# Adaptive-norm modulation in a 1-core block kernel: the two condition vectors become the stationary operand, the weights stream 512 wide, and three norm sums move between the weight tiles

## What is computed

```python
# end of the first block
x = x + 0.5 * swiglu_ffn(rmsnorm(x, norm_ffn2), ffn2_w_in, ffn2_w_out)
x = rmsnorm(x, norm_final)
# start of the second block; c is the condition of x, c_ctx that of ctx (256 positions)
m_x = split(silu(c)     @ mod_w + mod_b, 6)      # mod_w is 1024 x 6144
m_c = split(silu(c_ctx) @ mod_w + mod_b, 6)
h_x = rms_norm(x,   norm1_g) * (1.0 + m_x[1]) + m_x[0]
h_c = rms_norm(ctx, norm1_g) * (1.0 + m_c[1]) + m_c[0]
z_x = h_x @ w_in
z_c = h_c @ w_in
# then a recurrent mixer, neighbourhood attention, a merge, and 16 routed experts (top 2)
```

## Time and profile before

| what | value |
|---|---|
| median of 3 runs | 4668.71 us |
| the profiled execution's own time | 4666.49 us |
| its span, first to last instruction | 4664.9 us |
| PE busy | 3958.7 us (85%), 16948 instructions |
| PEld busy | 2824.8 us (61%) |
| DVE, ACT, POOL busy | 1965.5, 1160.9, 915.5 us |
| mean granted TensorE clock | 0.864 of full |
| modulation, L903: 768 matmul rows | 164.0 us |
| HBM read and written | 362.01 MB, 33.03 MB |

### The profile page before, as it was taken

One profiled execution on the slowest core, in us unless ns is written; L12 is line 12 of the kernel. 1 busy time (PEld: TensorE's weight loads), 2 busy tenths in 40 slices (PEclk: granted clock), 3 DMA queues, 4 the chain that ended last, 5 costly groups with the idle time before them and its releaser, 6 DMA issues.

```text
span 4664.9 us, 48689 instructions
## 1 busy us (share of the span) xinstructions
PE 3958.7 (85%) x16948; PEld 2824.8 (61%) x16948; DVE 1965.5 (42%) x2791; ACT 1160.9 (25%) x1552; POOL 915.5 (20%) x513
## 2 busy tenths in 40 slices
PE   8998888677499989999798766588898979969996
PEld 6875555333144458789454444587888864457775
DVE  2101554588600021100201333656666550159997
ACT  4421443323200033310101122111111010046663
POOL 4442000000000024420000000101101000049996
PEclk9999999888799999985898555788888979979998
DMA  2224111111022222234111000000000002349996
GB/s 102 94 89 172 45 45 40 39 51 49 19 76 76 73 70 92 90 127 153 50 59 45 9 18 25 1 0 0 0 0 0 0 0 89 110 172 357 358 356 242
DMA packets 106808, 395.84 MB, mean 85 GB/s; under 512 B 11680, under 2 KB 11696, under 8 KB 106112
## 3 DMA queue, kind: packets, MB, share of 16 engines
q1 hardware_dynamic: 95040, 347.42, 21.4%
q0 software_dynamic: 8400, 35.61, 2.0%
q10 hardware_dynamic: 3312, 12.06, 0.6%
HBM read 362.01 MB, written 33.03 MB: 85 GB/s over the span
## 4 chain that ended last, share of the span: by engine, by line
PE 67%; DVE 21%; issue 7%; ACT 3%; DVEq 1%; POOL 1%; DMA 1%; ACTq 0%; POOLq 0%; SPq 0%; PEldq 0%
PE psum L1379 9%; PE psum L827 7%; PE psum L197 5%; PE psum L196 5%; PE psum L198 5%; DVE er_r L1885 5%; PE psum L459 4%; DVE mem L775 4%; PE psum L903 4%; PE psum L945 3%; PE psum L1703 2%; PE psum L1097 2%; PE psum L469 1%; PE psum L1079 1%; PE psum L834 1%
## 5 line engine op out<-in xcount | busy, mean ns | idle before, releaser
L186 POOL TENSOR_TENSOR ring_r<-ring,whi 128x1024 fp32r<-128x1024 f32 x132 | 319.4, 2436 | 924.9 <-ACT whi L181 924.9
L1379 PE MATMUL psum<-mem 128*128 128x128 f32 x3520 | 462.3, 295 | 4.4
L1379 PEld LDWEIGHTS psum<-mem 128*128 128x128 f32 x3520 | 446.0, 210 | 16.9 <-DVE mem L1559 11.5
L1885 POOL TENSOR_TENSOR er_r<-er,eh 128x1024 fp32r<-128x1024 f32 x134 | 426.0, 3216 | 50.2 <-ACT eh L1873 50.2
L1885 DVE TENSOR_TENSOR er_r<-er,eh 128x1024 fp32r<-128x1024 f32 x134 | 367.8, 2784 | 0.0
L196 PE MATMUL psum<-ffn_xh,ring_r 128*128 128x512 f32 x704 | 279.3, 397 | 24.7 <-DVE xn_r L210 24.7
L681 PE MATMUL psum<-xn,ring 128*128 128x512 f32 x512 | 238.1, 629 | 69.2 <-ACT mem L717 64.8
L197 PE MATMUL psum<-ffn_xh,whi 128*128 128x512 f32 x704 | 281.2, 399 | 0.0
L198 PE MATMUL psum<-xn_r,whi 128*128 128x512 f32 x704 | 279.2, 397 | 0.0
L1873 ACT ACTIVATE eh<-er 128x1024 fp32r<-128x1024 f32 x268 | 262.5, 1071 | 10.0 <-DMA er<-experts 9.4
L681 PEld LDWEIGHTS psum<-xn,ring 128*128 128x128 f32 x512 | 103.0, 203 | 204.2 <-issue 199.0
(11 more groups left out here) (458 smaller groups left out, 6904.5 us busy)
## 6 DMA issues: line engine op xcount, KB each, us to landing
ring<-stream SPq DMA_DIRECT2D x359, 512.0 KB, 3.3
er<-experts SPq DMA_DIRECT2D x276, 512.0 KB, 6.0
xs_dram<-zero_row POOLq DMA_DIRECT2D x1, 12288.0 KB, 38.3
xs<-xs_dram SPq DMA_DIRECT2D x23, 512.0 KB, 6.6
ys_dram<-y_t ACTq DMA_DIRECT2D x23, 512.0 KB, 6.4
mem<-rpb POOLq DMA_DIRECT2D x8, 512.0 KB, 4.4
resid<-x_t SPq DMA_DIRECT2D x1, 2048.0 KB, 7.8
spill<-resid POOLq DMA_DIRECT2D x1, 2048.0 KB, 6.6
```

Source lines behind the costliest of these rows:

```text
L186: pool.tensor_tensor(ring_r[:, s, :, :], ring[:, s, :, :], f(whi[:, s, :, :]), ALU.subtract).then_inc(w_lo, 1)
L1379: ins = pe.matmul(psum[:, bank, q * n:(q + 1) * n], lhs[:, q, :], rhs if rhs is two_ident else rhs[:, q, :], start=True, stop=True)
L1885: eng.tensor_tensor(er_r[:, at, :], er[:, at, :], f(eh[:, at, :]), ALU.subtract).then_inc(done, 1)
```

## The change

It changes the modulation's product and what surrounds it, in six places:

- **Roles.** The two conditions are now stationary (128 rows, 2 columns) and 512 columns of weights move. There are 12 groups of 4 slabs; each group gives a 2 x 512 row in PSUM bank 0 or 1, by turns, from 8 products. The host lays the 48 slabs out anew (same size and number).
- **Rows to columns.** ACT copies each 2 x 512 row to `modrow` (L939). When all 12 are there, PE turns them by 48 transposes into bank 6 (L918), where DVE finds them as before.
- **Earlier start.** PE waits for the second of DVE's 8 additions to `resid`, not the eighth.
- **Sums between groups.** `norm_pe(pe, 3)` stands after 2 groups, `norm_pe(pe, 4)` and the context's sums (now L930) after 7. ACT's squares and roots and DVE's reciprocals are put in matching places.
- **Interleaved norm.** `mod_norm_dve` writes its additions between its multiplications, for norm 4 and for norm 5; the reciprocal is its own function, `rstd_dve`.
- **Finer waits.** The first `in2` tile waits for `xn` tile by tile, and the wait for the context's `hc` stands at the first tile that reads it.

```diff
-        def mod_pe(pe):
-            pe.wait_ge(resid_ready, 3 * DT)
-            pe.wait_ge(cs_dve, 1)
-            with pe.Fori(0, 12) as i:
-                for j in range(4):
-                    w = use_slab(pe, "mod", j, i, 4)
-                    for k in range(DT):
-                        ins = pe.matmul(psum[:, 6, bass.ds(i * 8 + 2 * j, 2)], w[:, k, :], cs[:, k:k + DT + 1:DT],
                                         start=k == 0, stop=k == DT - 1)
                     ins.then_inc(slab_used, 1)
+        def mod_rows(pe, groups):
+            for n in groups:
+                if n >= 2:
+                    pe.wait_ge(row_act, n - 1)
+                for j in range(4):
+                    w = use_slab(pe, "mod", 4 * n + j).rearrange("p a c -> p (a c)")
+                    for kk in range(2):
+                        k = 2 * j + kk
+                        ins = pe.matmul(psum[0:2, n % 2, :], cs[:, k:k + DT + 1:DT], w[:, kk * T:(kk + 1) * T],
+                                        start=k == 0, stop=k == DT - 1)
+                    ins.then_inc(slab_used, 1)
+        def mod_turn(pe, groups):
+            for n in groups:
+                pe.wait_ge(row_act, n + 1)
+                for m in range(4 * n, 4 * n + 4):
+                    ins = pe.transpose(psum[:, 6, 2 * m:2 * m + 2], modrow[:, m * P:(m + 1) * P], ident[0:2, 0:2])
+            return ins
+        def mod_and_norms_pe(pe):
+            pe.wait_ge(resid_ready, 2 * DT + 2)
+            pe.wait_ge(cs_dve, 1)
+            mod_rows(pe, (0, 1))
+            norm_pe(pe, 3)
+            mod_rows(pe, range(2, 7))
+            norm_pe(pe, 4)
...
+            ins.then_inc(cn_pe, 1)
+            mod_rows(pe, range(7, 12))
+            mod_turn(pe, range(12)).then_inc(turned, 1)
+        def mod_and_norms_act(act):
+            def take(groups):
+                for n in groups:
+                    act.wait_ge(slab_used, SLAB_AT["mod"] + 4 * n + 4)
+                    act.activation(modrow[:, n * T:(n + 1) * T], psum[0:2, n % 2, :], ACT.Copy).then_inc(row_act, 1)
...
         def block2_pe(pe):
-            norm_pe(pe, 4)
...
-            pe.wait_ge(xn_ready, 5 * DT)
-            pe.wait_ge(cn_dve, 1 + 2 * DT)
...
+                        if t == 0:
+                            pe.wait_ge(xn_ready, 4 * DT + k + 1)
...
+                        if u == 0:
+                            pe.wait_ge(cn_dve, 1 + 2 * DT)
...
         def block2_dve(dve):
-            dve.wait_ge(slab_used, SLAB_AT["mod"] + 48)
+            rstd_dve(dve, 4)
+            dve.wait_ge(cn_act.sem, cn_act.at(0, "std"))
+            dve.reciprocal(stdc, stdc).then_inc(cn_dve, 1)
+            dve.wait_ge(turned, 1)
```

More of the change, by code:

```diff
@@ L893, in hybrid_block_kernel @@
         spilled = sem("spilled")
-        def mod_pe(pe):
-            pe.wait_ge(resid_ready, 3 * DT)
-            pe.wait_ge(cs_dve, 1)
-            with pe.Fori(0, 12) as i:
+        modrow = mem[0:2, 0:48 * P]
+        row_pe = sem("mod_row_pe")
+        row_act = sem("mod_row_act")
+        turned = sem("mod_turned")
+        def mod_rows(pe, groups):
+            for n in groups:
+                if n >= 2:
+                    pe.wait_ge(row_act, n - 1)
                 for j in range(4):
-                    w = use_slab(pe, "mod", j, i, 4)
-                    for k in range(DT):
-                        ins = pe.matmul(psum[:, 6, bass.ds(i * 8 + 2 * j, 2)], w[:, k, :], cs[:, k:k + DT + 1:DT],
+                    w = use_slab(pe, "mod", 4 * n + j).rearrange("p a c -> p (a c)")
+                    for kk in range(2):
+                        k = 2 * j + kk
+                        ins = pe.matmul(psum[0:2, n % 2, :], cs[:, k:k + DT + 1:DT], w[:, kk * T:(kk + 1) * T],
@@ L904, in mod_pe @@
                                         start=k == 0, stop=k == DT - 1)
                     ins.then_inc(slab_used, 1)
-        def mod_norm_dve(dve, n, gain, shift):
+        def mod_turn(pe, groups):
[11 more added lines that the diff above has]
+            norm_pe(pe, 4)
+            for j in range(DT):
+                pe.wait_ge(cn_act.sem, cn_act.at(0, f"q{j}"))
+                ins = pe.matmul(psum[:, 5, 0:TC], ones[:, :], sqc[:, j, :], start=j == 0, stop=j == DT - 1)
+            ins.then_inc(cn_pe, 1)
+            mod_rows(pe, range(7, 12))
+            mod_turn(pe, range(12)).then_inc(turned, 1)
@@ new lines, in mod_and_norms_act @@
+        def mod_and_norms_act(act):
[3 more added lines that the diff above has]
+                    act.activation(modrow[:, n * T:(n + 1) * T], psum[0:2, n % 2, :], ACT.Copy).then_inc(row_act, 1)
+            act.wait_ge(resid_ready, 3 * DT)
+            for j in range(DT):
+                act.activation(xn[:, j, :], resid[:, j, :], ACT.Square).then_inc(sq_ready, 1)
+            take((0, 1))
+            act.wait_ge(sum_ready, 4)
+            act.activation(std[:, :], psum[:, 7, :], ACT.Sqrt, bias=eps[:, 0:1], scale=1.0 / D).then_inc(std_ready, 1)
+            take((2, 3, 4))
+            act.wait_ge(ctx_in, 16)
+            for j in range(DT):
+                act.activation(sqc[:, j, :], hc[:, j, :], ACT.Square).then_inc(cn_act.sem, 1)
+            for j in range(DT):
+                act.wait_ge(xn_ready, 3 * DT + j + 1)
+                act.activation(xn[:, j, :], resid[:, j, :], ACT.Square).then_inc(sq_ready, 1)
+            take((5, 6))
+            act.wait_ge(sum_ready, 5)
+            act.activation(std[:, :], psum[:, 7, :], ACT.Sqrt, bias=eps[:, 0:1], scale=1.0 / D).then_inc(std_ready, 1)
+            act.wait_ge(cn_pe, 1)
+            act.activation(stdc, psum[:, 5, 0:TC], ACT.Sqrt, bias=eps[:, 0:1], scale=1.0 / D).then_inc(cn_act.sem, 1)
+            take(range(7, 12))
@@ new lines, in mod_norm_dve, with scaled, shifted @@
+        def mod_norm_dve(dve, n, gain, shift):
+            def scaled(j):
+                dve.scalar_tensor_tensor(xn[:, j, :], resid[:, j, :], gain(j), std[:, :], ALU.mult, ALU.mult).then_inc(mid, 1)
+            def shifted(j):
+                dve.wait_ge(mid, DT * (n - 4) + j + 1)
+                dve.tensor_scalar(xn[:, j, :], xn[:, j, :], shift(j), None, ALU.add).then_inc(xn_ready, 1)
+            scaled(0)
+            for j in range(1, DT):
+                scaled(j)
+                shifted(j - 1)
+            shifted(DT - 1)
@@ L909, in mod_norm_dve, with rstd_dve @@
+        def rstd_dve(dve, n):
             dve.wait_ge(std_ready, n + 1)
@@ L911, in mod_norm_dve @@
             dve.wait_ge(rstd_ready, n + 1)
[L912 to L916, removed]
         def block2_pool(pool):
@@ L969, in block2_act @@
         def block2_act(act):
[L970 to L975, removed]
             act.wait_ge(xn_ready, 5 * DT)
@@ L997, in block2_dve @@
             mod_norm_dve(dve, 4, lambda j: gm1[:, j, 0:1], lambda j: modv[:, j, 0:1])
-            dve.wait_ge(cn_act.sem, cn_act.at(0, "std"))
-            dve.reciprocal(stdc, stdc).then_inc(cn_dve, 1)
             dve.wait_ge(cn_dve, 1)
@@ L2208, in moe_dve @@
         def moe_dve(dve):
+            rstd_dve(dve, 5)
             mod_norm_dve(dve, 5, lambda j: gm2[:, j:j + 1], lambda j: modv[:, 3 * DT + j, 0:1])
@@ L2307, in _ @@
             ffn_act(act, 1)
-            norm_act(act, 3, 24)
+            mod_and_norms_act(act)
             block2_act(act)
@@ L2320, in _ @@
             ffn_pe(pe, 1)
-            mod_pe(pe)
-            norm_pe(pe, 3)
+            mod_and_norms_pe(pe)
             block2_pe(pe)
@@ L2425, in lay_out @@
     ffn(i["ffn2_w_in"][0], i["ffn2_w_out"][0])
-    parts.append(k_slabs(i["mod_w_2"][0]))
+    parts.append(i["mod_w_2"][0].reshape(4, 2, P, 12, T).transpose(3, 0, 2, 1, 4).reshape(48, P, SLAB, P))
     in2 = i["w_in_2"][0]
```

## The result

| | median us | lowest to highest | runs |
|---|---|---|---|
| before | 4668.88 | 4668.22 to 4669.26 | 4 |
| changed | 4564.29 | 4560.86 to 4565.88 | 4 |

The ratio is 0.9778, with a 95% interval of 0.9766 to 0.979. The forecast of 4642.8 with half clock was wrong by 78.5 us. The first rival, full clock at 4565, is what happened; the range held the result, but only because that rival was in it.

What follows compares the result with a forecast made beforehand. Bound: a serial chain through modulation and norms to in2, PE often standing. 2060.8 + 155.2 + 23.0 + 10.8 + 2.5 + 9.0 = 2261.3 for the first in2 tile's end, against 2287.2: 25.9 us gained, 4642.8 us; range 4557 to 4656.

Steps and rivals of the forecast that it cites:

- half clock: Likeliest case: the modulation's rows run at 1.2 GHz apart from carried-over stretches; 4642.8 us, own range 4634 to 4656, chance 0.53.
- first rival: Modulation's rows keep full clock to their end, 82.4 us; first in2 tile ends at 2183.2, 4565 us in all; chance 0.41.
- The rows: Modulation's 192 instructions: 82.4 us at full clock, 164.9 at half; half taken, 155.2 us after carry-over.
- Carry-over: Full clock outlasts wide work before the rows by mean 3.6 us; 9.7 us at full clock over three stretches.
- Start: PE waits for 2 of 8 additions, so the modulation starts at 2060.8 rather than 2064.77: 4.0 us gained.
- The sums: Sums of norms 3 and 4 and context stay on PE: twice 9.6 and 3.7, 23.0 us, as before.
- Row copies: ACT's copies of modulation rows out of PSUM are covered by the groups: cost 0, or 7 us if cover failed.
- The transposes: 48 transposes after the modulation, paced by the load of 128 columns: 10.8 us at half clock, 5.4 at full.
- To the first product, first tile: From transposes to the first in2 product 2.5 us; then the first in2 tile takes 9.0, against 8.7 before.
- DMA: Modulation's slabs: 0 at half clock; in the full-clock rival 3 us (0 to 7) for masks and context.
- The norms: Norms 3 and 4: PE's standing between sums goes, covered by weight groups; without cover they would cost 49.8 us again.
- The slower rival: Rows at half clock, stationary load and array fill not overlapped, 38 us more: 4681 us; chance 0.06.

Runs made afterwards that it cites:

- e3: e2's kernel, with PE also waiting before the product for all of resid, masks and context to land, so the clock is down at its start: 4582.85 us.
- e5: e3's kernel with 64 of 128 rows in the modulation's product, half of the sum over channels left out: 4663.34 us.
- e8: e3's kernel with a stationary operand of 64 rows by 128 columns, of ones instead of the conditions: 4659.67 us.
- e7: Changed kernel, sums between the groups, with 32 of 128 rows in the modulation's product: 4634.26 us.
- e4: Changed kernel with the context's load put behind the modulation's second group and the masks' load behind its last: 4559.05 us.
- e2: Changed kernel with the three sums and all the norms' work put back after the whole new product, in the old order: 4572.62 us.
- e9: Kernel before, with only the finer waits and interleaved norm 4 of the change; product and order of the norms stay old: 4649.24 us.
- e6: Changed kernel, sums between the groups, with 64 of 128 rows in the modulation's product: 4595.87 us.
- e1: Changed kernel with the old product and its wait for all of resid; norms moved between weight groups, finer waits and interleaved norm 4 kept: 4640.91 us.

## Why the prediction was wrong

**The rows: the step that failed.** "A stationary of 2 columns uses far less of the array still. So I take half clock for the rows." The term was 155.2 us; 90.9 was measured, slab waits included, and nearly all of it at 1.00. The bounds of 82.4 and 164.9 us were right, and the value taken was at the wrong one of them. The nearest row was of the attention's scores, with fewer *rows* of the array (64 of 128). I carried what it shows over to fewer *columns*. e3, e5 and e8 show that the two are not alike: 64 rows in place of 128 kept the clock down, 2 columns in place of 128 did not. The row was weak evidence besides: under half of its 7.1 us were products of 64 rows, and PE stood 2.4 us on either side.

The Trainium skill's "TensorE: Matmul & The Clock Gate", section "What's actually happening", says that activity releases the throttle. That gave the right side for this change, and e3 agrees (0.50, then 1.00 about 4 us into the product). Read without regard to rows it fails in e5, where PE is busy for 19.96 of 20 us and the clock stays at 0.50 to the product's end.

**Carry-over.** There was none to count, as the clock didn't fall with the product. That a full clock outlasts the work that raised it is right: e7 shows it, with 5 to 6 us where I had taken 3.6.

**Start.** 2060.8 expected, 2060.98 measured.

**The sums.** 23.0 us expected, 7.07 + 7.06 + 3.45 = 17.6 measured, as the full-clock rival had it (17.5): they begin at full clock now.

**Row copies.** Hidden, as expected; L939 never stands in the chain.

**The transposes.** 10.8 us expected (8 in the rival), 3.07 measured, 64 ns each. I took the duration of a load for the pace. L1091 also moves 128 columns, these move 2. At half clock, in e5, they take 5.21 us, still half of what I took.

**To the first product, first tile.** 2.5 and 9.0 expected, 2.6 (2172.52 to 2175.08) and 9.3 (36.76 - 27.48) measured.

**DMA.** The rival's 3 us for masks and context were 7: 4.1 us of waiting and, which no term had, the clock at 0.50 for 6.7 us behind it, which costs half of that. e4 takes both away with the two loads. With a later wait of about 1 us the product took 90.9 us where 82.4 is its pace. This was 5.5 us more than the rival had, and the transposes were 4.9 us less. That the two cancelled is luck, and is why the rival's end of the first tile, 2183.2, is so near 2184.4.

**The norms.** 26 us of standing had been named as what goes, and I put it down to the groups as a cover: "Without that cover the two norms would cost their 49.8 again". That is wrong. e2 and e9 show 29.5 and 30.5 us without any cover. Most of it went through the finer waits, and the moved sums are worth only 7 to 9.

**The slower rival.** It doesn't hold: in e5, at half clock, an instruction of L909 lasts 1.057 us (median) and they follow each other every 0.854, so the load of the stationary and the fill are overlapped.

## What to carry to other kernels

For a product of a few vectors with a large matrix, make the vectors stationary and move the weights 512 wide with all 128 partitions filled: here, in float32 on one core, the clock then stood as high as in `in2`. When a nearby row of a profile is used for a new shape, ask in which of its dimensions it is near. Before work is moved to hide a serial norm, let each step wait for the one tile that it reads; here this, with the interleaved norm, gave 20 us and the moving 7 to 9.

## What the runs showed of the hardware

- Two products that keep PE busy without a gap can stand at different clocks for their whole length: 128 rows by 2 columns at 1.00 (34 of 34 us), 64 rows by 128 or by 2 columns at 0.50 (164 us), both with 512 moving columns.
- 64 rows hold a full clock for 34 us, but don't win it back once it has fallen behind a slab wait of 0.80 us, and stay at 0.50 for the remaining 46, which costs 23 us (e6). 128 rows kept 1.00 through a wait of 0.90 us at the same place, and lost it for 6.7 us behind one of 2.69.
- Loads of 128 x 128 weights for 2 moving columns each don't raise the clock: 56 us with PE and PEld busy for all of it at 0.50 (e1).
- 48 transposes of 2 rows by 128 columns follow each other every 64 ns at full clock (3.07 us) and every 109 ns at half (5.21 us, e5).
